# A 1024-token hybrid decoder trunk: half of the last delta head's gate projection is computed beside that head's own first steps, and the output weights are split sooner

## The reference

```python
def gdn_mixer(x, w_in, conv_w, a_log, dt_bias, norm_g, w_out):
    h = x @ w_in                                   # q, k, v, z of 8 heads, and beta, decay
    qkv = silu(causal_depthwise_conv(qkv, conv_w))
    q, k = l2_normalize(q), l2_normalize(k)
    o = gated_delta_rule(q, k, v, beta, g)         # chunks of 64, a triangular solve in each
    o = rms_norm(o, norm_g) * silu(z)              # z is the head's gate
    return o.reshape(B, S, GDN_V) @ w_out
```

## Time and profile before

| | us |
|---|---|
| median of 3 runs | 1793.45 (1791.71 to 1794.51) |
| profiled execution, its own time | 1791.22 |
| its span, first to last instruction | 1789.5 |
| PE busy, share of the span | 1700.4, 95% |
| DVE, ACT, POOL busy | 866.6, 789.3, 309.0 |
| mean granted TensorE clock | 0.979 |

### The profile page before, as it was taken

How to read it: one execution, slowest core, us unless ns; L and a number is a source line. 1 busy time by engine, 2 the same in 40 slices (tenths; PEclk the granted TensorE clock), 3 DMA queues, 4 the chain that set the end, 5 groups by cost and what they waited for, 6 DMA issues and landing times. The chain is left out here.

```text
span 1789.5 us, 28862 instructions
## 1 busy us (share of the span) xinstructions
PE 1700.4 (95%) x11199; PEld 1297.2 (72%) x11199; DVE 866.6 (48%) x1656; ACT 789.3 (44%) x1288; POOL 309.0 (17%) x243
## 2 busy tenths in 40 slices
PE   9999999999999897899989998999999999898998
PEld 6777777777777675678877887666666665686786
DVE  5647667575675536553332100344444444565433
ACT  4646466464564623142222311556555665430411
POOL 5213212132121432200000000222221221012000
PEclk9999999999999998989999999999999999999899
DMA  6211011210101221041130201111111101040311
GB/s 156 49 37 44 17 49 22 51 37 25 49 21 52 69 74 60 25 140 45 39 108 24 72 2 47 36 45 31 45 42 36 42 22 39 32 158 24 118 45 51
DMA packets 113079, 92.86 MB, mean 52 GB/s; under 512 B 19696, under 2 KB 95664, under 8 KB 112944
## 3 DMA queue, kind: packets, MB, share of 16 engines
q1 hardware_dynamic: 112944, 91.02, 17.7%
HBM read 82.51 MB, written 8.49 MB: 51 GB/s over the span
## 5 line engine op out<-in xcount | busy, mean ns | idle before, releaser
L430 PE MATMUL gdn_unit<-part_hi,gdn_w_hi 128*128 128x512 f32 x496 | 226.0, 456 | 0.0
L432 PE MATMUL gdn_unit<-part_hi,gdn_w_lo 128*128 128x512 f32 x496 | 195.3, 394 | 0.0
L431 PE MATMUL gdn_unit<-part_lo,gdn_w_hi 128*128 128x512 f32 x496 | 194.6, 392 | 0.0
L2062 DVE CUSTOM_DVE_ANT_0 fa_probs<-fa_scores,fa_decay 128x896 f32<-128x896 f32 (+7 forms) x128 | 97.1, 758 | 120.3 <-PE fa_scores L1874 72.9
L848 DVE SCALAR_TENSOR_TENSOR x<-gdn_raw,gdn_taps,x 128x512 f32<-128x512 f32 x144 | 130.5, 907 | 32.6 <-ACT x L657 27.7
L1826 PE MATMUL fa_unit<-part_hi,fa_w_hi 128*128 128x512 f32 x256 | 115.0, 449 | 4.9 <-ACT fa_qk L1973 3.4
L394 POOL TENSOR_TENSOR gdn_w_lo<-ring,gdn_w_hi 128x1024 fp32r<-128x1024 f32 x31 | 75.2, 2427 | 238.9 <-ACT gdn_w_hi L637 238.9
L2008 ACT ACTIVATE fa_probs_t<-fa_turned 128x512 f32<-128x512 f32 (+1 forms) x96 | 52.3, 545 | 139.3 <-PE fa_turned L1891 138.8
L2002 ACT ACTIVATE fa_probs<-fa_probs,fa_top 128x896 f32<-128x896 f32 (+7 forms) x128 | 99.4, 777 | 22.6 <-DVE fa_top L2062 19.0
L432 PEld LDWEIGHTS gdn_unit<-part_hi,gdn_w_lo 128*128 128x128 f32 x496 | 93.2, 188 | 20.8
L1263 PE MATMUL e_gate<-e_w_hi,e_a_hi 128*128 128x512 f32 x256 | 103.2, 403 | 2.8 <-DVE e_a_lo L1400 2.8
(11 more groups left out here) (313 smaller groups left out, 3645.4 us busy)
## 6 DMA issues: line engine op xcount, KB each, us to landing
ring<-in_gdn_w_in_dram SPq DMA_DIRECT2D x32, 512.0 KB, 4.1
ring<-in_ple_w_gate_dram SPq DMA_DIRECT2D x32, 256.0 KB, 3.0
ring<-in_fox_w_in_dram SPq DMA_DIRECT2D x32, 256.0 KB, 2.9
ring<-in_fox_w_in_dram SPq DMA_DIRECT2D x16, 512.0 KB, 4.7
fa_decay<-c_rows_scratch SPq DMA_DIRECT2D x64, 128.0 KB, 3.0
gdn_g_bc<-g_rows_scratch SPq DMA_DIRECT2D x8, 512.0 KB, 8.5
x_scratch<-x SPq DMA_DIRECT2D x8, 512.0 KB, 2.9
m_old<-x_scratch SPq DMA_DIRECT2D x8, 512.0 KB, 3.5
```

Of the source, the lines that this page charges most:

```text
L430: pe.matmul(out, w_hi[:, j % 2, k, :], xh[:, k, ts], start=(k == 0), stop=False)
L431: pe.matmul(out, w_hi[:, j % 2, k, :], xl[:, k, ts], start=False, stop=False)
L432: mm = pe.matmul(out, w_lo[:, j % 2, k, :], xh[:, k, ts], start=False, stop=(k == KT - 1))
```

## The change

The tables of steps change, a semaphore `late_passed` is new, and PE has a new function:

```diff
-TAKE_PARTS = (28, 30, 37, 44, 51, 58, 61)
-PART_FROM = 15
-O_PARTS = (10, 21, 31, 45)
-OUT_ROWS = tuple(range(10, 26, 2))
+TAKE_PARTS = (26, 28, 35, 42, 49, 56, 61)
+PART_FROM = 13
+O_PARTS = (6, 21, 31, 45)
+OUT_ROWS = (1, 3, 5, 9, 11, 13, 15, 18)
+LATE_FROM = 6 * KT
+LATE_STEPS = KT
+AT_LATE_TAKE = 2 * KT - LATE_STEPS
+AT_LATE_SILU = 40
...
+            def project_late(m):
+                k, u, j = m // 2, 6 + m % 2, 4 * H - 1
+                n = 8 * (H - 1) + u
+                if k == 0:
+                    pe.wait_ge(w_low, j + 1)
+                    pe.wait_ge(unit_taken, n - 1)
+                out, ts = unit[n % 2][:], slice(u % 2 * HALF, (u % 2 + 1) * HALF)
+                pe.matmul(out, w_hi[:, j % 2, k, :], xh[:, k, ts], start=(k == 0), stop=False)
+                pe.matmul(out, w_hi[:, j % 2, k, :], xl[:, k, ts], start=False, stop=False)
+                mm = pe.matmul(out, w_lo[:, j % 2, k, :], xh[:, k, ts], start=False, stop=(k == KT - 1))
+                mm.then_inc(unit_made if k == KT - 1 else late_passed, 1)
...
             def part_work(s):
-                if s == AT_FIRST - 1:
-                    pe.wait_ge(unit_taken, 8 * H)
-                    for n in range(20):
-                        pe.matmul(unit[n % 2][:, 0:P], c["ident"][:], c["tri"][:], start=True, stop=True)
+                if s < 2 * KT - LATE_STEPS:
+                    project_late(LATE_STEPS + s)
...
+                    if k == 0 and n < 2:
+                        pe.wait_ge(unit_taken, 8 * H - 1 + n)
...
-                    if it < H and 8 * it + s // KT >= 2:
+                    if it == H - 1 and s >= LATE_FROM:
+                        if s - LATE_FROM < LATE_STEPS:
+                            project_late(s - LATE_FROM)
+                    elif it < H and 8 * it + s // KT >= 2:
                         project(it, s)
...
                     k = OUT_ROWS.index(s)
+                    if k < KT - 1:
+                        act.wait_ge(late_passed, 2 * k + 2)
+                    else:
+                        act.wait_ge(unit_made, 8 * H)
                     act.wait_ge(out_loaded[k % 3], 16 * (k // 3 + 1))
                     step(act.activation(xh[:, k], out_raw(k), ACT.Copy), out_high)
...
-                    if it < H and s % 8 == 0 and s:
+                    if it < H and s % 8 == 0 and s and (it, s) != (H - 1, 7 * KT):
                         take_unit(it, s // 8 - 1)
+                    if it == H and s == AT_LATE_TAKE:
+                        take_unit(H - 1, 6)
+                        take_unit(H - 1, 7)
+                    if it == H and s == AT_LATE_SILU:
+                        z = qkvz[:, (H - 1) % 2, 3]
+                        step(act.activation(z, z, ACT.Silu), z_ready)
```

More of the change, by code:

```diff
@@ L259, in delta_net @@
         part_made, part_taken = sem("part_made"), sem("part_taken")
+        late_passed = sem("late_passed")
         block = ph.enter_context(nc.Block())
@@ L786, in _ @@
                         out_work(s)
-                if it < H:
+                if it == H - 1:
+                    v = qkvz[:, it % 2, 2]
+                    act.wait_ge(conv_made, 6 * it + 6)
+                    step(act.activation(v, v, ACT.Silu), v_ready)
+                elif it < H:
                     take_unit(it, 7)
```

2 lines of the change are left out of this document (added).

## The result

| | before | after |
|---|---|---|
| median, us (same chip, alternating; 4 runs each) | 1792.74 | 1803.93 (1802.58 to 1805.22) |
| ratio, 95% interval | | 1.0055 [1.0041, 1.0069] |
| profiled execution: own time, span | 1791.22, 1789.5 | 1805.22, 1803.5 |
| PE busy; mean granted clock | 1700.4; 0.979 | 1704.1; 0.973 |

What follows compares the result with a forecast made beforehand. PE was taken to bound the kernel, iteration 8 set by when PE may start the parts plus what stands behind. Terms +2.36, +1.38, -0.35, -0.26 and +1.13 gave +4.26 us: 1797.7 us on the median, range 1793.0 to 1801.0.

Steps and rivals of the forecast that it cites:

- The chain from the sums on: Iteration 8: head 6's sums, ACT's root, exponential and silu, w_out row 0, POOL's list, then PE's first part.
- The step that failed first: Head 6's sums (L503): PE arrives about 2.7 us sooner but still waits for POOL until 596.08, leaving an idle gap.
- fifth term: Head 6's sums behind the new 2.7 us idle gap: lower PE clock costs +1.13 us, from 0 to 1.92.
- first term: Start of the parts: the heads' low part stands behind other work in POOL's list, so PE starts +2.36 us later.
- other sum of 5.1: Total if contention with DVE also slowed POOL's list by two hand-overs of 0.42: 5.1 instead of 4.3 us.
- second term: Between PE's first part and the levels' first product: two triples more, +1.38 us.
- fourth: PE's wait for the first part taken: now behind level 4 instead of level 5, with shorter DVE work, -0.26 us.
- third: End of the iteration, s = 60: two triples fewer give back what the tail waited for them, -0.35 us.
- After the 1.85 us wait the windows show 1.00 throughout: price 0: Wait before the first part taken, used as lower bound for the clock's price in the new gap at the sums: 0.
- ACT's list: Rival: inside the levels ACT waits in order for w_out rows to land, 1 to 3 us on top, 1799.7 us; chance 0.16.
- The parts really fill the wait: Rival: at the start of the parts the 4.43 us wait and low clock go, -5.7 us, 1787.8 us; chance 0.09.

Runs made afterwards that it cites:

- The repair of the order: Changed kernel with the late triples reordered so that the first triple into the bank ACT has yet to empty comes one step later: 1801.93 us, 1.0046.
- POOL order run: Changed kernel with the heads' low part moved to s = 1, ahead of the rows of w_out: 1805.38 us, 1.0070.
- the late projection alone: Changed kernel's late gate projection with the four step tables of the kernel before: 1796.64 us, 1.0024.
- both lists mended: Changed kernel with the heads' low part at s = 1 and the last five rows of w_out later in ACT's list: 1799.43 us, 1.0025.
- The halves of the change: Two kernels: changed kernel with the old step tables, 1796.64 us; kernel before with the new step tables only, 1797.64 us.
- the filling: Changed kernel with seven constant matmuls in PE's wait for the first part taken, in the levels: 1799.49 us, 1.0036.
- The filling at the tail: Changed kernel with 18 constant matmuls behind the last triple of the delta net (s = 62): 1801.16 us, 1.0041.
- the reordered version: Changed kernel with twelve late triples in iteration 7, four in 8, bank-repair order, heads' low part and row 0 first, other steps moved: 1789.39 us, 0.9980.

## Why the prediction was wrong

**The chain from the sums on and its direction held.** The idle time ahead of the sums is 2.48 us (2.5 to 2.8 forecast), released by POOL; four POOL instructions without a gap ahead of the heads' low part; PE's first part directly behind it; L581 5.34 us behind the first part (5.4 forecast); the wait for the first part taken 1.62 us (1.6); L926 behind ACT's root.

**The step that failed first**: "L503 waits for POOL until 596.08, which nothing in the change moves". The change moved it by 2.24 us. The two late units share the step, and unit 7 goes into the bank that unit 61 has just finished in and that ACT has not taken. Before, a new unit began eight steps behind the last one in its bank. PE waited 2.17 us at the second late triple with head 6's last chunks of the state behind it in its list, and ACT's take of them, POOL's square and the sums came later by that. The prediction looked at the late triples as work that is gone from ahead of the sums, not at what their new order waits for. The order of before and after showed `unit_taken` in `project_late`; the rows to price it with (when ACT takes a unit) were in the timeline of ACT. The repair of the order took back 1.2 of the 2.2 us; that the rest is the same wait is read from the trace (0.97 us of it were left), not from an edit.

**The clock in the new gap (fifth term, 1.13)** was 1.73 in the profile, and 1.45 to 1.5 by the two edits that removed it, within its bounds of 0 to 1.92. Mechanism right, size low by half a microsecond. But with the bank repaired the gap of 2.48 us had no drop, and behind gaps of 2.46 to 2.49 us the sums took 2.61 us in the POOL order run and 3.11 with the late projection alone. The price of 1.13 came from a row that itself takes between 1.98 and 3.68 us from one execution to the next, behind the same wait. So the comparison by length of wait was luck, and only the bounds held.

**POOL's list (first term, 2.36)** was 2.74. Of the 0.4 more, 0.3 is POOL's own (12.07 us from the first row's start to the low part's end, for 11.8 forecast; the first row took 2.49 us while DVE worked on the block inverse), and 0.1 the step from POOL's end to PE. The Trainium skill (GPSIMD Engine Reference, section 8, Key points) speaks of contention with VectorE on a shared interface; the trace agrees, with two instructions of DVE at 2.45 us for 0.42 and POOL's 0.05 to 0.1 us each. The loss falls nearly all on DVE, so the prediction's other sum of 5.1 was too much, and DVE had slack in the changed kernel. With POOL's order mended it hasn't: PE then waits for the inverse until 618.91 (both lists mended).

**Two triples (second term, 1.38)** cost 1.27 in this profile. Over the eight traces with the parts at s = 13 behind POOL's low part the way from the first part to the levels is 5.2 to 6.3 us, by how long the lower clock lasts, so the 0.5 us either way that the prediction allowed was narrow. The **first take (fourth, -0.26)** gave 0.23, the **tail (third, -0.35)** some 0.3.

**"After the 1.85 us wait the windows show 1.00 throughout: price 0"** was used for the new gap and never asked of that wait's own place in the changed kernel. There the wait, now 1.62 us, was followed by the low clock for 6.8 us, +2.9 us. A shorter wait did what a longer one had not. The halves of the change show that this goes with the new tables: they put the wait behind level 4 instead of level 5, and 23.3 us behind the first part (649.61 - 626.29) instead of 25.9 (644.78 - 618.93). What in that decides isn't settled; the filling shows only that with PE busy there the drop goes.

**The end was drawn at the barrier.** The third term looked at DVE's L889 and stopped there. PE had fewer triples at s = 60, idled 6.01 us instead of 4.91 into the barrier, and took 1.4 us more behind it. The filling at the tail took that back and 1.4 us more.

**The rivals.** "ACT's list" had 0 and took 0 in the changed kernel; with POOL's order mended alone it took back all of the 3.8 us gained and 2.7 more, by PE's waits and the clock behind them. "The parts really fill the wait" needed `o_low` by 614.5: the reordered version has it by 609.5, and is faster than before. The sum was 4.26 for 11.8: 2.24 for the bank, 0.6 for the clock at the sums, 0.4 for POOL, 2.9 for the levels and 1.4 behind the barrier are the difference; the small terms cancel within 0.1.

## What to carry to other kernels

When work is moved on the bounding engine, price not only what it leaves behind but what it waits for at its new place: two accumulations side by side need both banks at once, and the one just finished is the last to be free. A wait on PE costs its length and may then cost the clock behind it, and each stretch behind a wait must be priced by itself, the barrier at the end included, as a range and not by one row of the same length; matmuls of constants in the gap are the cheap test of that. And a row split early is worth nothing when it stands ahead of the one tile that the next engine waits for.

## What the hardware showed that I had not expected

- A DVE `tensor_tensor` with two SBUF operands of 64x256, 0.42 us, took 2.45 us when it began after a POOL `tensor_tensor`, and ended 0.28 us behind that one. The six of these eight ahead of it took 0.42 us each; the sixth had begun 0.14 us before POOL's (613.94 and 614.08). POOL's own instruction beside them took 2.49 us, for 2.37 to 2.40 otherwise.
- Equal waits of PE had different sequels. At the sums of head 6: 2.48 us with the low clock behind it (the sums took 3.65 us), 2.46 us with less of it (2.61 us, the POOL order run) and 2.48 us without (1.96 us, the bank's repair). In iteration 0, where nothing differs between the kernels: 3.19 to 3.24 us in all 14 traces, and 1.98 to 3.68 us for the same four matmuls behind it.
- 1.6 us of wait was followed by the lower clock in all eight traces that have it (for 6.8 us in the changed kernel), while 1.85 us was not in either of two.
- Two of the kernels with half the change, and the one with both lists mended, had times in two groups with 4 to 5 us between their middles, on the same chip and in the same minutes.
